# Linear attention, gate product and head norms as steps under the memory key and value tiles, output projection as tiles of each token group

## The chip, the core and the metric

The kernel runs on one core of a Trainium2 chip (trn2). The metric is the device time of one execution in microseconds; lower is better. TensorE (PE, with its weight loads PEld) multiplies, VectorE (DVE), ScalarE (ACT) and GpSimd (POOL) work element by element, SyncE (SP) issues most transfers. Each engine takes its instructions strictly in the order in which the program lists them and waits at semaphores for the others.

## What is computed

A two-layer encoder over two token groups, a prompt group of 512 tokens ("P") and a sample group of 256 ("S"), with 1024 channels and shared weights. Cut to what matters:

```python
def trunk(x, mem, p):                      # both groups, all in float32
    # layer 0: mixer = S5 state space | gated linear attention (GLA)
    u, q, k, v, og, glr = split(rms_norm(x) @ ev_w_in)
    y_s5  = s5_mixer(u, ...)               # ends: y = gelu(y); y * sigmoid(y @ w_glu)
    y_gla = gla_mixer(q, k, v, og, glr)    # two directions, chunks of 64, 4 heads of 64 x 128
    x = x + concat(y_s5, y_gla) @ ev_w_out                     # output projection
    x = x + cross_attention(rms_norm(x), rms_norm(mem), ...)   # 256 memory tokens a group, 4 heads
    x = x + square(relu(rms_norm(x) @ w1)) @ w2                # MLP, 1024 -> 4096 -> 1024
    # layer 1: differential attention, then cross attention and MLP again

def gla_mixer(...):
    g = log_sigmoid(lr @ w_gate + b_gate) / 16                 # a decay per direction and channel
    # per chunk: b = cumsum(g);  scores = tril((q e^(b-ref)) (k e^(ref-b))^T)
    #            o = scores v + (q e^b) S_prev;   S = e^(b_last) S_prev + (k e^(b_last-b))^T v
    return rms_norm(o, per head) * silu(og)
```

## The kernel before

Channels lie on the 128 partitions, tokens along the rows. A **tile** of work is one 128x128-column block of a weight matrix (512 KB) against all tokens of a group: 24 matmuls, because values and weights are split into a high and a low part and three of the four products are taken (`pe_tile`, L1757). Each weight tile is loaded by SyncE, copied to its high part by ScalarE (`high`, L1729) and subtracted to its low part by VectorE (`low`, L1734). A prompt tile has 512 moving columns, a sample tile 256.

The program has three stages, each of one or more blocks; at the end of a block all engines meet.

- `mixer_in`: the combined input projection (17 tiles) woven with the state-space mixer in four batches (`NB`). q, k, v and gates are parked in DRAM, the mixer's output y too (`store_y`, L540), and loaded back at its end (L827, L828); x is loaded again (L830).
- `s5_gla`, in blocks one after the other: the gate product (L1072, with wglu), then linear attention for the head pairs t = 0 and 1 over all 768 tokens (gates L1164, cumulative sum L1204, transposes of k L1173, chunk states L1182 and their recurrence L1225, scores L1277, masks L1302, head outputs L1285 and L1290), the sigmoid of the output gates (L1318), `head_norm_stage`, and the output projection as `product_stage` with its own weight stream (L249, L251). GpSimd does the products of q and decay (L1236) and low parts of weights (L218).
- `trunk_tail`: a list of **slots** written out at build time. A slot holds one tile, or none, and steps of other work that were queued with `later`; `drain` empties the queue into slots without a tile. Every engine walks the same list. On TensorE a slot is: scores of attention steps, the tile, the statistic of the tile before (`pe_post`), then the other steps; on ScalarE and VectorE: first parts of steps, the weight part two or three tiles ahead, the tile's evacuation (`act_tile`, `dve_tile`), the statistic of the tile before (`dve_post`, L2044 to L2046), last parts of steps. The tail begins with the sample group's cross norm, then its query tiles, memory keys and values of layer 0 (16 tiles on the 512 memory tokens, `memory(m0)`), output tiles, memory of layer 1 (16 tiles), then the sample MLP with the prompt group's query tiles and cross attention inside it, and the prompt MLP.

Norm steps have the granularity of `FINE` or `PAIRS` (channels per slot): apply (`dve_apply`, L2120), high part on ScalarE, residue on VectorE (`dve_fin`, L2127).

## Time and profile before

| | us |
|---|---|
| median of three runs (2866.41 to 2869.27) | 2867.13 |
| the profiled execution | 2867.88 |
| its span | 2866.1 |
| TensorE busy (x14044) | 2539.3, 89% |
| VectorE busy (x2658) | 1562.5, 55% |
| ScalarE busy (x1896) | 1128.5, 39% |
| GpSimd busy (x24) | 42.0, 1% |
| TensorE's share of the chain that ended last | 65% |

The span runs from the first to the last instruction of the profiled execution; the 1.8 us around it belong to the time. A matmul's busy time overlaps its neighbours', so a busy TensorE isn't one at its peak. The granted clock is the share of full speed that TensorE's clock had, one of the two levels 0.5 and 1.0 at any moment, and a mean over a window.

### The profile page before, as it was taken

Reading aid. Unit: us, or ns where it says so; the run is one execution under the profiler, and the core shown is the slowest. Engines: PE = TensorE matmul, PEld = TensorE weight load, DVE = VectorE, ACT = ScalarE, POOL = GpSimd, SP = SyncE. Lnnn points to the kernel's source line nnn. Section 1 sums busy time; section 2 is a strip of 40 time slices with the busy share of each in tenths; the row PEclk is TensorE's granted clock in tenths of the full one; section 3 lists DMA queues with packets and bytes.
Section 4 is the critical chain, followed back from the end, with each engine's and each line's share of the span. In section 5 each row is a group of like instructions: output and inputs, shape, how many; then the busy total and the mean of one; then the engine's idle time right before and its main releaser. Section 6 shows DMA issues by size and latency. Waiting matters only on the chain.

```text
span 2866.1 us, 35043 instructions
## 1 busy us (share of the span) xinstructions
PE 2539.3 (89%) x14044; PEld 2162.3 (75%) x14044; DVE 1562.5 (55%) x2658; ACT 1128.5 (39%) x1896; POOL 42.0 (1%) x24
## 2 busy tenths in 40 slices
PE   5887356656999999999999999999989999999999
PEld 3786235645878789988997798877777789888887
DVE  8798354153546555556646654465577555543333
ACT  4131011122434444535545544354556444343332
POOL 0000011020000000000000000000000000000000
PEclk9899665578999999999999999999999999999999
DMA  4222500002323432533442242322322332333332
GB/s 139 78 65 61 186 3 0 0 29 80 96 74 118 140 103 89 178 118 125 132 133 81 82 155 88 110 89 81 96 75 81 125 118 89 112 116 96 96 99 92
DMA packets 96481, 274.34 MB, mean 96 GB/s; under 512 B 18080, under 2 KB 32544, under 8 KB 94912
## 3 DMA queue, kind: packets, MB, share of 16 engines
q1 hardware_dynamic: 94016, 261.62, 29.4%
q10 hardware_dynamic: 2304, 10.49, 1.2%
q8 instruction: 112, 1.84, 0.3%
q14 instruction: 49, 0.40, 0.0%
HBM read 254.77 MB, written 15.20 MB: 94 GB/s over the span
## 4 chain that ended last, share of the span: by engine, by line
PE 65%; DVE 6%; ACT 3%; issue 1%; DMA 0%; SPq 0%; ACTq 0%; DVEq 0%
PE ps L1757 57%; PE ps L1823 2%; PE ps L1850 2%; PE ps L1892 1%; DVE wlo L1734 1%; PE ps L1868 1%; PE ps L1881 1%; ACT whi L1729 1%; PE ps L1789 1%; DVE ringP L2120 1%; DVE region_S L2173 1%; DVE ps L2045 1%; DVE ps L2044 0%; DVE region_S L2192 0%; DVE yP L2046 0%
## 5 line engine op out<-in xcount | busy, mean ns | idle before, releaser
L1734 DVE TENSOR_TENSOR wlo<-wraw,whi 128x1024 fp32r<-128x1024 f32 x416 | 505.2, 1218 | 54.8 <-ACT whi L1729 54.7
L1757 PE MATMUL ps<-in_hP,whi 128*128 128x512 f32 x1280 | 516.4, 403 | 2.5 <-issue 2.5
L1729 ACT ACTIVATE whi<-wraw 128x1024 fp32r<-128x1024 f32 x416 | 437.5, 1052 | 178.8 <-PE ps L1757 134.0
L1757 PE MATMUL ps<-in_hP,wlo 128*128 128x512 f32 x1280 | 500.1, 391 | 0.0
L1757 PE MATMUL ps<-in_lP,whi 128*128 128x512 f32 x1280 | 499.2, 390 | 0.0
L1757 PE MATMUL ps<-in_hS,whi 128*128 128x256 f32 x1024 | 306.4, 299 | 24.5 <-DVE in_lS L2127 14.8
L1757 PE MATMUL ps<-in_lS,whi 128*128 128x256 f32 x1024 | 293.8, 287 | 0.0
L1757 PE MATMUL ps<-in_hS,wlo 128*128 128x256 f32 x1024 | 293.1, 286 | 0.0
L1757 PEld LDWEIGHTS ps<-in_hP,whi 128*128 128x128 f32 x1280 | 241.0, 188 | 58.9 <-issue 8.8
L1757 PEld LDWEIGHTS ps<-in_lP,whi 128*128 128x128 f32 x1280 | 241.1, 188 | 53.7 <-issue 5.5
L1757 PEld LDWEIGHTS ps<-in_hP,wlo 128*128 128x128 f32 x1280 | 240.8, 188 | 51.9
L2065 DVE TENSOR_TENSOR x<-ps,x 128x512 f32<-128x512 f32 (+1 forms) x176 | 98.1, 557 | 314.8 <-PE ps L1757 313.7
L1757 PEld LDWEIGHTS ps<-in_hS,whi 128*128 128x128 f32 x1024 | 200.4, 196 | 42.8 <-issue 19.8
L1757 PEld LDWEIGHTS ps<-in_lS,whi 128*128 128x128 f32 x1024 | 200.8, 196 | 2.8 <-issue 2.0
L1757 PE MATMUL ps<-hid_hP,whi 128*128 128x512 f32 x512 | 202.1, 395 | 0.0
L1757 PEld LDWEIGHTS ps<-in_hS,wlo 128*128 128x128 f32 x1024 | 200.4, 196 | 0.0
L1757 PE MATMUL ps<-hid_hP,wlo 128*128 128x512 f32 x512 | 199.3, 389 | 0.0
L1757 PE MATMUL ps<-hid_lP,whi 128*128 128x512 f32 x512 | 199.3, 389 | 0.0
L2075 DVE TENSOR_TENSOR hid_lP<-ps,hid_hP 128x512 fp32r<-128x512 f32 x64 | 44.3, 692 | 234.6 <-ACT hid_hP L1969 234.6
L1967 ACT ACTIVATE ps<-ps 128x512 f32<-128x512 f32 (+1 forms) x128 | 60.7, 475 | 261.7 <-PE ps L1757 261.5
L1757 PE MATMUL ps<-hid_hS,whi 128*128 128x256 f32 x512 | 149.7, 292 | 9.2 <-DVE hid_lS L2075 5.8
L1757 PE MATMUL ps<-hid_lS,whi 128*128 128x256 f32 x512 | 145.7, 285 | 0.0
(434 smaller groups left out, 4146.5 us busy)
## 6 DMA issues: line engine op xcount, KB each, us to landing
wraw<-wt SPq DMA_DIRECT2D x416, 512.0 KB, 3.5
mix_wraw<-wt ACTq DMA_DIRECT2D x12, 512.0 KB, 4.2
raw<-wstream SPq DMA_DIRECT2D x4, 1024.0 KB, 11.0
x<-x_in SPq DMA_DIRECT2D x4, 768.0 KB, 8.5
vog<-vog_scratch SPq DMA_DIRECT2D x1, 3072.0 KB, 14.1
x<-x_in SPq DMA_DIRECT2D x1, 3072.0 KB, 12.0
mix_wraw<-wt SPq DMA_DIRECT2D x5, 512.0 KB, 10.3
mix_u<-x SPq DMA_DIRECT2D x32, 64.0 KB, 3.0
```

Of the source, the lines that this page charges most:

```text
L1729: nc.scalar.activation(whi[:, n % NHI, :, :], wraw[:, n % NRAW, :, :], ACT.Copy).then_inc(wh.sem, 1)
L1734: nc.vector.tensor_tensor(wlo[:, n % NRAW, :, :], wraw[:, n % NRAW, :, :], whi[:, n % NHI, :, :].bitcast(F32), ALU.subtract).then_inc(wr.s ...
L1757: last = nc.tensor.matmul(ps[:, m % 2, 0:N[prod.g]], w_[:, k, :], x_[:, k, :], start=(k == 0 and j == 0), stop=(k == KT - 1 and j == 2))
L1789: nc.tensor.matmul(ps[:, 2, 0:s.n], s.mat, ring[g][:, i % 2, :], start=True, stop=True).then_inc(z["ssum"].sem, 1)
L1823: last = nc.tensor.matmul(ps[:, 3 + q_ % 2, b * 256:(b + 1) * 256], qx[g][:, 2 * h + j, lo:lo + P], km[g][:, 2 * h + j, :], start=(j == 0) ...
L1850: last = nc.tensor.matmul(ps[:, 7, j * 256:(j + 1) * 256], vm[g][:, kt, (2 * h + j) * P:(2 * h + j + 1) * P], at[:, q_ % 2, kt * 256:(kt + ...
L1868: last = nc.tensor.matmul(ps[:, 3 + zz, 0:N[g]], dq[g][rows, h, b * P:(b + 1) * P], dk[g][rows, h, :], start=True, stop=True)
L1881: last = nc.tensor.transpose(ps[:, 5, j * P:(j + 1) * P], scb[g][:, q_ % 2, 0, j * P:(j + 1) * P], ident)
L1892: last = nc.tensor.matmul(ps[:, 6 + h % 2, b * P:(b + 1) * P], dv[g][:, j, h * P:(h + 1) * P], at[:, q_ % 2, j * P:(j + 1) * P], start=(j ...
L1967: act_chain(nc.scalar.activation(acc_ps, acc_ps, ACT.Relu))
L2065: nc.vector.tensor_tensor(x[:, i, cols(g)], ps[:, b, 0:N[g]], x[:, i, cols(g)], ALU.add).then_inc(tf[b].sem, 1)
L2075: nc.vector.tensor_tensor(hid_l[g][:, i, :], ps[:, b, 0:N[g]], hid_h[g][:, i, :].bitcast(F32), ALU.subtract)\
```

## The change

`s5_gla`, `product_stage`, `head_norm_stage` and all that served them are gone. `mixer_in` ends with the memory norm of layer 0 (squares and sums before the last mixer product, `dve_mem` behind it), issues the load of the memory and of the tail's first five weight tiles from ScalarE's queue after its last tile, and parks the low-rank gate input in DRAM too. The tail begins with the 16 memory tiles of layer 0, four slots without a tile, and the 16 memory tiles of layer 1. Linear attention is cut into four **units** (sample and prompt group, head pairs 0 and 1) of seven steps, one step a slot; the gate product into four groups of output columns with two steps each; each head's norm and gate into two steps. Keys and values of both layers now go through DRAM (`load_kv`). The output projection is eight sample and eight prompt tiles of the ordinary kind ("eo"); then come query tiles of both groups, output tiles, and the sample MLP's 64 tiles in one piece. From the prompt MLP of layer 0 on, the order is that of before.

```diff
-            nS, n0 = Norm("S", "cross0"), Norm("P", "mem0", mem, ymem)
-            later([("squares", nS)], *norm_steps(nS, PAIRS), [("squares", n0)])
-            drain()
-            q = Product("q", "S", WT["q0"], nS.ready)
...
+            m0 = Memory(0, None)
             memory(m0)
...
+            n1.after = m0
+            m1 = Memory(1, n1.ready)
+            scale = norm_steps(n1, PAIRS)
+            scale[0] = [("napply", n1, 0, 2)]
+            for st_ in scale[:4]:
+                slots.append((None, st_))
+            later(scale[4])
+            memory(m1)
+            gl = {g: Gla(g) for g in "SP"}
+            gl["P"].after = m1
+            units_ = [Unit(0, "S", 0, "A", 0), Unit(1, "S", 1, "A", 1536), Unit(2, "P", 0, "B", 0), Unit(3, "P", 1, "A", 0)]
+            for o in range(4):
+                attach(16 + o, [[("glu", o, 0)], [("glu", o, 1)], [("gsplit", gl["S"], o, o + 1)]])
+            for u, first in zip(units_, (1, 6, 20, 25)):
+                attach(first, [[("gla", u, k)] for k in range(7)])
+            attach(12, [[("ogload", "S", 2), ("wgluload",)]])
+            for h in range(GH):
+                attach(13 + 2 * h, [[("fin", gl["S"], h, 0)], [("fin", gl["S"], h, 1)]])
+            attach(31, [[("ogload", "P", 4), ("gsplit", gl["S"], 4, 6)], [("gsplit", gl["S"], 6, 8)], [("xload",)]])
+            for h in range(GH):
+                attach(32 + h, [[("fin", gl["P"], h, 0)], [("fin", gl["P"], h, 1)]])
+            nS = Norm("S", "cross0")
+            queue[0].append(("gsplit", gl["P"], 0, 2))
+            later(*[[("gsplit", gl["P"], k, k + 2)] for k in range(2, KT, 2)], [("kvload", "S", 0, None)], [("kvload", "P", 0, None)])
+            run(Product("res", "S", WT["eo"], gl["S"].ready, norm=nS))
+            nP = Norm("P", "cross0")
+            later([], *norm_steps(nS, PAIRS))
+            run(Product("res", "P", WT["eo"], gl["P"].ready, norm=nP))
+            q = Product("q", "S", WT["q0"], nS.ready)
+            later(*norm_steps(nP, FINE))
+            run(q)
+            qp = Product("q", "P", WT["q0"], nP.ready)
...
+            later([("qstat", q)], *cross_steps(a))
+            run(qp)
...
+            later([("qstat", qp)], *cross_steps(ap_))
+            run(Product("res", "S", WT["o0"], a.ready, norm=nS))
+            rest = [queue.popleft() for _ in range(len(queue))]
+            later(*merged(rest, norm_steps(nS, PAIRS)))
+            for _ in rest:
+                slots.append((None, queue.popleft()))
+            nP = Norm("P", "mlp0")
+            run(Product("res", "P", WT["o0"], ap_.ready, norm=nP))
             nS1 = Norm("S", "mix1")
             mS = Mlp("S", 0, nS, nS1)
...
             later([], *norm_steps(nP, FINE))
-            mS.run(16)
+            mS.run(64)
```

A unit's TensorE steps (the ScalarE and VectorE parts have the same step numbers, `act_gla` and `dve_gla`; the long middle part of step 1 comes behind the slot's tile, `act_gla_post` and `dve_gla_post`):

```diff
+            def pe_gla(pe, u, k):
+                if k == 0:
...
+                    for z in range(2):
+                        nc.tensor.matmul(ps[:, 3 + z, 0:u.n], wg[:, z, t * P:(t + 1) * P], lr[:, cols(g)], start=True, stop=True)\
+                            .then_inc(zd.sem, 1)
+                elif k == 2:
...
+                        pe.wait_ge(krd.sem, 2 * i + z + 1)
+                        for j in range(BL[g]):
+                            last = nc.tensor.transpose(ps[:, 5 + z, j * P:(j + 1) * P], u.krel[z][:, j * P:(j + 1) * P], ident)
+                elif k == 3:
+                    pe.wait_ge(ktr.sem, 2 * i + 2)
+                    pe.wait_ge(qrd.sem, 2 * i + 2)
+                    pe_scores(pe, u)
+                elif k == 4:
+                    pe.wait_ge(scr.sem, i + 1)
...
+                                last = nc.tensor.matmul(kv_ps(z, c)[DK * hh:DK * hh + DK], koT[rows, z, lo:lo + DK],
+                                                        vtok[g][rows, c // 2, h * DV:(h + 1) * DV], start=True, stop=True)
+                elif k == 5:
+                    pe.wait_ge(wrd.sem, i + 1)
+                    pe_heads(pe, u)
```

## Rows read from the trace of the kernel before

**Rows 1.** The page: busy tenths in 40 slices, and TensorE's granted clock
```profile
PE   5887356656999999999999999999989999999999
...
PEclk9899665578999999999999999999999999999999
```
**Rows 2.** Windows, stages up to 753 us: start:end, length, busy (count) by engine, PEclk, DMA share, GB/s
```profile
344.40:370.90 26.50, 22.93 (x64) 12.98 (x64) 8.46 (x8) 3.28 (x5) 0.04 (x1) 0.92 0.10 40
370.90:413.60 42.70, 13.53 (x116) 9.64 (x117) 28.13 (x38) 12.51 (x17) 13.00 (x12) 0.56 0.02 5
413.60:464.20 50.60, 46.59 (x192) 41.95 (x192) 3.78 (x4) 0.81 (x1) 0.00 (x0) 0.50 0.00 0
464.20:554.90 90.70, 59.27 (x308) 50.75 (x308) 31.91 (x42) 13.70 (x19) 9.62 (x4) 0.52 0.00 1
554.90:601.20 46.30, 11.65 (x16) 4.70 (x16) 21.64 (x24) 24.75 (x30) 0.00 (x0) 0.54 0.00 0
601.20:683.30 82.10, 71.38 (x384) 61.28 (x384) 27.11 (x24) 7.54 (x4) 19.17 (x4) 0.92 0.07 26
683.30:752.90 69.60, 41.55 (x237) 37.43 (x237) 42.56 (x70) 34.36 (x66) 0.00 (x0) 0.73 0.40 135
```
**Rows 3.** Windows of the tail, in the same columns
```profile
849.30:867.00 17.70, 10.79 (x50) 8.10 (x48) 7.53 (x15) 4.92 (x12) 0.00 (x0) 0.90 0.11 31
...
891.30:985.80 94.50, 94.50 (x423) 76.72 (x423) 48.83 (x78) 39.16 (x61) 0.00 (x0) 1.00 0.41 123
...
1080.10:1150.40 70.30, 68.61 (x458) 64.51 (x457) 41.93 (x74) 32.94 (x74) 0.00 (x0) 0.98 0.30 90
...
1222.40:1265.90 43.50, 43.50 (x194) 36.03 (x193) 17.34 (x21) 12.13 (x15) 0.00 (x0) 1.00 0.31 99
1265.90:1321.50 55.60, 49.47 (x387) 48.05 (x387) 40.36 (x58) 33.61 (x58) 0.00 (x0) 0.97 0.48 150
1321.50:2866.10 1544.60, 1503.49 (x8030) 1265.51 (x8028) 821.26 (x1404) 695.54 (x1218) 0.00 (x0) 0.99 0.33 102
1730.80:1791.90 61.10, 59.98 (x278) 50.10 (x277) 25.08 (x43) 24.06 (x47) 0.00 (x0) 1.00 0.23 70
1153.40:1222.40 69.00, 69.00 (x578) 69.00 (x577) 37.37 (x48) 34.65 (x51) 0.00 (x0) 1.00 0.60 183
```
**Rows 4.** Timeline around the mixer's end: start, length, instruction, [idle before <-releaser]
```profile
317.84 0.81 ACT L681 ACTIVATE sq<-ps 128x768 f32<-128x768 f32 x1 [40.23 <-PE ps L618]
...
321.25 0.96 DVE L782 SCALAR_TENSOR_TENSOR sq<-sq 128x768 f32<-128x768 f32 x1 [0.91 <-ACT sq L686]
...
344.39 2.07 PE L1072 MATMUL ps<-uqk,wglu_sb 128*128 128x512 f32 x2 [26.59 <-DMA wglu_sb<-wglu]
...
362.21 0.81 ACT L1084 ACTIVATE glu_t<-ps 128x768 f32<-128x768 f32 x1 [4.35 <-PE ps L1074]
```
**Rows 5.** Groups by line: xcount | busy us, mean ns of one | idle before
```profile
L1734 DVE TENSOR_TENSOR wlo<-wraw,whi 128x1024 fp32r<-128x1024 f32 x17 | 20.7, 1220 | 0.0
L2044 DVE SCALAR_TENSOR_TENSOR ps<-ps,yP 128x512 f32<-128x512 f32 x4 | 2.8, 700 | 17.8 <-ACT yP L1912 17.8
L2120 DVE SCALAR_TENSOR_TENSOR ringP<-region_P,par 128x512 f32<-128x512 f32 x8 | 5.8, 746 | 0.0
L2127 DVE TENSOR_TENSOR in_lP<-ringP,in_hP 128x512 fp32r<-128x512 f32 x8 | 5.3, 688 | 3.5 <-ACT in_hP L1984 3.3
L1204 DVE TENSOR_TENSOR_SCAN uqk<-gm,uqk 128x768 f32<-128x768 f32 x2 | 3.5, 1758 | 0.1
L1225 DVE SCALAR_TENSOR_TENSOR gl_b<-gl_b,decay,ps 128x128 f32<-128x128 f32 x40 | 11.6, 345 | 9.5 <-PE ps L1182 9.1
L1252 ACT ACTIVATE sq<-rstd 128x768 f32<-128x768 f32 x2 | 1.7, 827 | 0.0
```
**Rows 6.** Timeline of linear attention's matmuls on TensorE (rows are records, two to a matmul)
```profile
401.92 2.83 PE L1182 MATMUL ps<-vog,gl_b 64*64 64x128 f32 x48
...
413.61 5.46 PE L1277 MATMUL ps<-gl_b,krel 64*128 64x128 f32 x24 [6.61 <-PEq L1160]
```

More of the change, by code:

```diff
@@ L24 @@
 M = 512
[L25 to L28 removed]
 DEPTH = 2
 FB = 4
+NRAW = 5
+NT_MIX = 17
 EPS = 1e-6
@@ new lines, in c3, with pe_scores @@
+            def c3(a):
+                return a.rearrange("p (c i) -> p c i", i=CH)
+            def pe_scores(pe, u):
+                for z in range(2):
+                    for j in range(BL[u.g]):
+                        js = slice(j * P, (j + 1) * P)
+                        for hh in range(2):
+                            rows = slice(DK * hh, DK * hh + DK)
+                            last = nc.tensor.matmul(ps[:, 3 + 2 * hh + z, js], u.krel[z][rows, js], u.qrel[z][rows, js], start=True, stop=True)
+                last.then_inc(scd.sem, 1)
```

1125 lines of the change are left out of this document (490 added, 635 removed).

## The prediction

> **What bounds the kernel now.** I read the page's forty slices first. TensorE's row stands at 9 in nearly every slice from the eleventh on, and holds values of 3 to 8 from the fifth to the ninth; its granted clock dips to 5 to 7 in the same slices [rows 1]. So something sits between 290 and 700 us that is neither long matmul work nor at full clock.
>
> The timeline around it shows TensorE waiting 26.6 us, to 344.4 us, while the mixer's last output is stored and read back and the gate weight arrives [rows 4]. Windows cut at the stage borders tell the rest [rows 2]. The gate product takes 26.5 us. Linear attention runs from 370.9 to 554.9 us, in three windows with TensorE busy 13.5, 46.6 and 59.3 us at clocks of 0.56, 0.50 and 0.52. Gates and head norms follow, 46.3 us with 11.7 busy; then the output projection, 82.1 us; then the first norm of the tail and the sample group's query tiles, 69.6 us with 41.5 busy. Behind it the memory key and value tiles run with TensorE busy throughout at clock 1.00 [rows 3]. Inside one stage the next instruction waits for the engine before it, so no engine is the bound from 318 to 753 us; the sequence is.
>
> The second set of windows gives prices of work that stays [rows 3]. 24 sample tiles take 69.0 us, 2.88 us each, with 183 GB/s; eight prompt tiles take 43.5 us, 5.44 us each; sixteen memory tiles with their head statistics and transposes take 94.5 us, 5.9 us each. The tile list of before reaches the first tile of the prompt group's layer-0 MLP after 128 tiles, at 1321.5 us. From there both kernels run the same 288 tiles in the same order, for 1544.6 us [rows 3]. So I count both kernels to that point.
>
> **The change, step by step.** *Mixer end.* In both kernels VectorE's last step of the mixer ends at 322.2 us [rows 4]. New behind it is the memory norm's finish: a table load and Ln and Exp on ScalarE (an estimate of 3 us, from its pass of 0.83 us over 768 columns, [rows 5]), three VectorE passes of 0.70 us, then eight times an apply of 0.75 and a residue of 0.69 us [rows 5]: 3 + 2.1 + 11.5 us, to about 339 us. The squares and the eight sum matmuls of that norm lie in the 40.2 us in which ScalarE waits for the mixer's last product [rows 4]: nothing. Without that cover they would cost about 8 x 1.1 us. ScalarE's six new DMA issues (memory, five weight tiles) lie in the same wait, and SyncE's queue loses the loads of x, q, k, v and the gate's halves there. Gone from the path are the read back [rows 4], which now has the whole first memory product as cover, and the norm and the weight loads after 683.3 us. Five weight tiles are loaded already, so the first tile needs a table load, one high part and one low part (1.2 us each by the low part's row, [rows 5]), and it runs on a TensorE that was idle: first tile as if started at 345 us.
>
> *Tiles that stay tiles.* 32 memory tiles, 2 x 94.5 = 189 us.
>
> *Linear attention's matmuls.* TensorE was busy 13.5 + 46.6 + 59.3 = 119.4 us with them, at about half clock [rows 2]; at full clock 60 us. The new form has the same products, less those at the sequence edges. Value 59 us, since they now stand between tiles that run at 1.00; the other end is 118 us, if they stay at half clock.
>
> *Its VectorE and ScalarE work.* By widths from [rows 5] a prompt unit (512 columns) holds VectorE for two scans of 1.17, some sixteen passes of about 0.65, twelve state steps of 0.35 and two wide multiplications of 1.2: about 20 us; a sample unit about 11 us. Together 62 us, beside some 45 us that 16 memory tiles themselves want (48.8 us in a window of 94.5 with a norm beside, [rows 3]). ScalarE needs less. Neither is full; what counts is who waits. Each unit is seven steps in seven tile slots, and TensorE's instruction of a step stands behind that slot's tile, so a step has 5.4 us of cover. Most steps fit. The third does not: its transposes wait for k times its decay, and between the gate product and that lie bias, minimum, Exp, Ln, subtraction, scan, differences, two Exp, product, with the tile's own evacuation and statistics queued between them on both engines. For a prompt unit I sum 16 us after the gate product, against two tiles of 5.6 us: 5 us of wait. Where the slot in between also holds a key tile's head statistic on VectorE (three passes of 0.70, [rows 5], and four half-width gains, some 4 us) the wait is 10; so it is for the first sample and the second prompt unit. Waits of 6, 1, 5 and 10 us, and 2 us for each prompt unit's state chain before its head products: 26 us. Behind a waiting TensorE stand the next tiles; behind VectorE's waits stand the low parts of weights, which are issued two tiles ahead.
>
> *Head norms and gates.* Eight sum matmuls of 0.43 or 0.85 us at full clock, 5 us, and about 1 us for each in which bank 2 is not free: 13 us.
>
> *Gate product.* Four no-tile slots between the two memory products hold it. Its four groups of matmuls follow each other every 5.16 us at full clock (0.81 + 4.35, [rows 4]): 20.6 us, with the second memory norm, the sample group's norms and the sigmoid on ScalarE beside it, and about 5 us until the first tile's last input: 26 us.
>
> *Clock.* Where TensorE has waited the granted clock may fall and the next tile start slow. The gate product's start after 26.6 us of waiting cost 26.5 - 20.6 = 6 us [rows 2, 4]; for waits of 5 to 10 us I take a third of it, an estimate, and count six: 12 us (0 to 36).
>
> *Projections, queries and cross attention.* Output projection as sample tiles 23 us, plus 7: in four of them VectorE has a low part of 1.22, two residues of 0.69 and two passes of 0.4 to do, 3.4 us for a tile of 2.88, and once a head norm of 4 us: 30. As prompt tiles 44. Sample query tiles with the prompt norm beneath, where VectorE is as full: 29. Prompt query tiles with sample cross attention beneath: the same pair took 61.1 us in layer 1 [rows 3], plus 3 for the queries' sums: 64. Sample output tiles with prompt cross attention: the twelve tiles of before with it took 70.3 us [rows 3]; here eight tiles and three empty slots, 52 + 18 (the drain of before, [rows 3]): 70. Prompt output tiles 44. The sample MLP's 64 tiles, 184 us, plus 10 for the norm steps under its first tiles, as the 16 tiles of before show (55.6 against 46.1 us, [rows 3]): 194. Sum 475 us.
>
> **Sum:** 345 + 189 + 59 + 26 + 13 + 26 + 12 + 475 = 1145 us, against 1321.5: a gain of 176 us. The profiled execution took 2867.9 us against a median of 2867.1, so I take **2691 us**.
>
> **A rule weighed.** From 413.6 to 464.2 us TensorE was busy 46.6 of 50.6 us and the granted clock stood at 0.50 throughout, the lower of its two levels, 1.2 of 2.4 GHz [rows 2]. So linear attention's own matmuls, dense as they are, didn't raise it in this stage; the gate product ran at 0.92 and the tile stages at 1.00 [rows 2, 3]. The Trainium skill, "TensorE: Matmul & The Clock Gate", section "HAM oscillation — how this bites in real kernels", puts slow clocks down to idle gaps between bursts. By that rule alone this stretch would have been fast, which the row contradicts. By the row the units' share would stay slow under the tiles as well, 59 us more than my sum.
>
> **The rivals.** *Chains not covered.* VectorE and ScalarE are in order, and a step of linear attention that waits holds the tile's evacuation too. If the 62 us of VectorE and some 28 us of ScalarE work (about 34 full passes of 0.83 us, [rows 5]) were all seen by TensorE, 90 us of waiting stand in place of 26: 2755 us. For it: in the present stage every one of these steps is seen [rows 2]. Against: in the memory windows VectorE works 48.8 of 94.5 us, so it has room [rows 3]. Half-clock units give about the same, 2691 + 59 = 2750.
>
> *Matmuls in pairs.* 48 matmul records of 64 rows and 64 columns took 2.83 us and 24 records of 64 rows and 128 columns 5.46 us, all over 128 moving columns and within 12 us [rows 6]: 0.05 against 0.22 us each. The new order alternates the two heads' row halves. If these ran two at a time, half of about 40 us at full clock would go, and with waits halved the time is 2691 - 20 - 20 = 2651 us. The Trainium skill, "TensorEngine Tiling (Array Packing)", section "Tiling Modes", says that row halves work in parallel, and also that a change of mode drains the array; what such a change costs no row here shows.
>
> *Slower: the clock stays low.* If the mix of tiles and small matmuls holds TensorE at the lower level from 345 to 670 us, all TensorE work there doubles: 189 + 59 + 21 + 5 = 274 us more, 2965 us. It decides once more than 176 of these 274 us lie at the low level. Against: cross attention's small matmuls between tiles ran at 0.98 [rows 3].
>
> *The change doesn't hide anything.* If the in-order queues make each slot last as long as its chain, the 184 us of linear attention remain on the path and only the gaps go (26.6 us of read back, [rows 4], 40 of the norm stage and 15 of the projection, [rows 2]): 2786 us, still faster.
>
> **Chances.** Forecast 0.60 (its own range 2660 to 2725), chains or half clock 0.22, pairs 0.10, nothing hidden 0.05, low clock 0.03. The range that leaves out no more than 2 in 10: 2645 to 2755. Faster by over 0.2% (5.7 us, about what a measurement of this kernel tells from no change) 0.96, within 0.01, slower 0.03.
>
> **What the profile after would show.** The first tile starts near 343 us; the first 16 memory tiles last about 120 us and the second 16 about 160; between them a gap of about 26 us holds the gate product; the first tile of the output projection starts near 670 us and the prompt MLP of layer 0 near 1145. Waits of TensorE for VectorE's product of k should stand at the head of its waits in those stretches, and GpSimd should have no work. I am wrong if the memory stretches last over 350 us together, if their granted clock is below 0.9, or if the tiles behind 670 us take over 500 us, as the new order of cross attention or the loads of x and of keys and values (7 MB in few tiles) may make them.

## The result and the profile after

| | before | after |
|---|---|---|
| median, us | 2866.77 (2866.39 to 2869.27, 4 runs) | 2669.94 (2669.03 to 2670.89, 4 runs) |
| span of the profiled execution, us | 2866.1 | 2667.4 |
| TensorE busy | 89% | 93% |

The ratio is 0.931, with a 95% interval from 0.930 to 0.933: 197 us less. The forecast was 2691 us with a range from 2645 to 2755. The page of the changed kernel, first its span, the busy times, and the rows of the forty slices that answer to [rows 1]:

```profile
span 2667.4 us, 35145 instructions
PE 2467.6 (93%) x14026; PEld 2099.6 (79%) x14026; DVE 1561.9 (59%) x2747; ACT 1147.3 (43%) x1975; POOL 0.2 (0%) x4
PE   5888489888999889999999999999989999999999
PEclk9899789999999999999999999999999999999999
```

The holes between slices five and eleven are filled, and TensorE's clock no longer dips to 5 there. GpSimd has next to no work (0.2 us). The windows are cut at the first matmul of each stage's first tile (columns: window, its length, then busy time and instructions of TensorE, weight load, VectorE, ScalarE and GpSimd, granted clock, DMA share, GB/s). In order: first memory product with the two sample units; the gap with the gate product; second memory product with the two prompt units; output projection, sample and prompt; sample queries; prompt queries with the sample group's cross attention; sample output with the prompt group's; prompt output; the sample MLP; all the rest.

```profile
341.70:466.70 125.00, 118.86 (x612) 95.34 (x613) 64.97 (x127) 45.12 (x84) 0.00 (x0) 0.93 0.42 138
466.70:497.00 30.30, 24.94 (x80) 14.39 (x78) 20.52 (x36) 18.03 (x35) 0.00 (x0) 0.94 0.14 44
497.00:652.40 155.40, 136.00 (x822) 106.89 (x821) 100.21 (x168) 66.09 (x112) 0.00 (x0) 0.93 0.34 107
652.40:678.10 25.70, 24.55 (x199) 23.76 (x198) 22.21 (x35) 17.05 (x27) 0.00 (x0) 1.00 0.62 212
678.10:722.10 44.00, 44.00 (x196) 36.41 (x195) 25.23 (x42) 17.22 (x27) 0.00 (x0) 1.00 0.48 173
722.10:754.70 32.60, 28.56 (x207) 27.69 (x206) 25.61 (x34) 18.40 (x33) 0.00 (x0) 0.90 0.41 130
754.70:817.00 62.30, 62.30 (x302) 52.91 (x301) 23.88 (x40) 22.52 (x46) 0.00 (x0) 1.00 0.22 68
817.00:885.10 68.10, 59.49 (x364) 54.32 (x363) 41.61 (x83) 27.83 (x66) 0.00 (x0) 0.95 0.22 70
885.10:928.80 43.70, 43.70 (x194) 36.19 (x193) 21.22 (x30) 13.45 (x19) 0.00 (x0) 1.00 0.27 85
928.80:1122.60 193.80, 186.51 (x1539) 184.95 (x1538) 115.05 (x154) 108.63 (x178) 0.00 (x0) 1.00 0.56 174
1122.60:2667.40 1544.80, 1503.83 (x8030) 1266.23 (x8028) 820.81 (x1404) 695.37 (x1218) 0.00 (x0) 0.99 0.32 102
```

The last row stands against the 1544.6 us of [rows 3]: from the prompt group's layer-0 MLP on nothing changed. All of the gain lies ahead of that point, which came at 1321.5 us and now comes at 1122.6. In the first and third row the clock is 0.93, where linear attention alone had 0.50 to 0.56 [rows 2], though VectorE works 165 of 280 us there. TensorE's waits between 341 and 665 us (engine, line <- releaser: total, times, longest):

```profile
PE ps L1863 <- DVE region_S L1943: 10.7, 2, 6.6
PE ps L1863 <- DVE x L1943: 4.8, 1, 4.8
PE ps L2015 <- DVE yP L1603: 4.0, 1, 4.0
PE ps L1828 <- DVE region_S L1966: 3.4, 3, 2.1
...
PE ps L2015 <- DVE vtmp L1654: 2.7, 3, 1.2
```

At the head stand the transposes of a unit's third step (L1863), which wait for the product of k and its decay on VectorE (L1943), as the prediction named them. Four units have three such waits, of 4.1, 4.8 and 6.6 us; the second sample unit has none. Third is a head norm's sum, then the head products (L1828, a unit's sixth step) that wait for the states. Left out is the first tile's wait for its weight, 2.8 us.

### The profile page after: what moved, and what is told of

The parts are those of the page before. It is cut to its first block, busy times and chain, and to the rows that moved or that the text cites. A ratio compares the mean times of both kernels' runs of the same rounds, so it can differ in the third digit from the quotient of the medians.

```text
span 2667.4 us, 35145 instructions
## 1 busy us (share of the span) xinstructions
PE 2467.6 (93%) x14026; PEld 2099.6 (79%) x14026; DVE 1561.9 (59%) x2747; ACT 1147.3 (43%) x1975; POOL 0.2 (0%) x4
## 4 chain that ended last, share of the span: by engine, by line
PE 74%; DVE 9%; ACT 4%; issue 1%; ACTq 0%; DVEq 0%
PE ps L1321 63%; PE ps L1384 2%; PE ps L1409 2%; DVE wlo L1298 1%; PE ps L1451 1%; PE ps L1427 1%; PE ps L1440 1%; DVE ps L1602 1%; DVE ps L1601 1%; PE ps L1353 1%; DVE yP L1603 1%; PE ps L1828 1%; ACT yP L1470 1%; DVE region_S L1726 1%; ACT whi L1293 1%
## 5 line engine op out<-in xcount | busy, mean ns | idle before, releaser
L1321 PE MATMUL ps<-in_hP,whi 128*128 128x512 f32 x1344 | 546.9, 407 | 4.4 <-DVE wlo L1298 2.8
L1298 DVE TENSOR_TENSOR wlo<-wraw,whi 128x1024 fp32r<-128x1024 f32 x432 | 524.1, 1217 | 36.7 <-ACT whi L1293 36.4
L1293 ACT ACTIVATE whi<-wraw 128x1024 fp32r<-128x1024 f32 x432 | 454.1, 1052 | 192.5 <-PE ps L1321 133.4
L1321 PE MATMUL ps<-in_hP,wlo 128*128 128x512 f32 x1344 | 527.6, 393 | 0.0
L1321 PE MATMUL ps<-in_lP,whi 128*128 128x512 f32 x1344 | 527.2, 392 | 0.0
L1321 PE MATMUL ps<-in_hS,whi 128*128 128x256 f32 x1088 | 321.5, 296 | 8.1 <-DVE hid_lS L1634 4.3
L1321 PE MATMUL ps<-in_lS,whi 128*128 128x256 f32 x1088 | 310.4, 285 | 0.0
L1321 PE MATMUL ps<-in_hS,wlo 128*128 128x256 f32 x1088 | 310.1, 285 | 0.0
L1321 PEld LDWEIGHTS ps<-in_hP,whi 128*128 128x128 f32 x1344 | 255.2, 190 | 67.1 <-issue 10.4
L1624 DVE TENSOR_TENSOR x<-ps,x 128x256 f32<-128x256 f32 (+1 forms) x192 | 106.8, 556 | 334.9 <-PE ps L1321 333.6
L1321 PEld LDWEIGHTS ps<-in_lP,whi 128*128 128x128 f32 x1344 | 255.4, 190 | 56.5 <-issue 5.3
## 6 DMA issues: line engine op xcount, KB each, us to landing
mix_mem<-mem_in ACTq DMA_DIRECT2D x1, 2048.0 KB, 10.4
```

The lines of the kernel that those rows point to most:

```text
L1293: nc.scalar.activation(whi[:, n % NHI, :, :], wraw[:, ws(n), :, :], ACT.Copy).then_inc(wh.sem, 1)
L1298: nc.vector.tensor_tensor(wlo[:, ws(n), :, :], wraw[:, ws(n), :, :], whi[:, n % NHI, :, :].bitcast(F32), ALU.subtract).then_inc(wr.sem, 1)
L1321: last = nc.tensor.matmul(ps[:, m % 2, 0:N[prod.g]], w_[:, k, :], x_[:, k, :], start=(k == 0 and j == 0), stop=(k == KT - 1 and j == 2))
L1624: nc.vector.tensor_tensor(x[:, i, cols(g)], ps[:, b, 0:N[g]], x[:, i, cols(g)], ALU.add).then_inc(tf[b].sem, 1)
```

## The experiments

All times are medians, each kernel beside runs of the kernel before on the same chip; its ratio to that has an interval of about ±0.0013, some 4 us. The changed kernel ran a second time in the midst of them (`e5_changed_again`: 2670.7 us), so a difference is taken against 2670.

> The changed kernel as it is, once more, as the measure for the three beside it: 2670 us by every theory.

The stage times are from the timelines of the profiled executions, each the distance between the first matmuls of two tiles, in us:

| kernel | median | first tile at | first memory product and gap | second memory product | output projection | MLP of the prompt group to the end |
|---|---|---|---|---|---|---|
| changed | 2669.9 | 341.7 | 155.3 | 155.4 | 69.7 | 1544.8 |
| changed, second run | 2670.7 | 341.2 | 155.3 | 155.4 | 69.7 | 1542.4 |
| e1 halves in turn | 2696.1 | 342.6 | 162.0 | 175.3 | 69.7 | 1544.2 |
| e2 spare slot | 2677.5 | 340.4 | 151.2 | 159.5 | 76.4 | 1544.9 |
| e3 no prompt units | 2617.7 | 341.8 | 155.3 | 107.1 | 69.7 | 1545.1 |
| e4 units uncovered | 2755.2 | 341.9 | 289.2 | 108.9 | 67.6 | 1544.9 |
| e6 sample units shifted | 2656.8 | 340.4 | 142.7 | 157.9 | 69.7 | 1542.2 |
| e6b prompt unit too | 2664.4 | 343.0 | 147.6 | 156.0 | 69.7 | 1544.2 |
| e7 prompt units early | 2656.8 | 340.6 | 147.5 | 150.4 | 67.6 | 1545.1 |
| e8 head norms back | 2660.3 | 342.2 | 145.6 | 154.8 | 69.7 | 1546.0 |
| e9 scan before statistic | 2650.0 | 342.7 | 145.3 | 148.6 | 69.7 | 1542.2 |
| e10 both | 2653.8 | 342.3 | 144.9 | 152.4 | 69.7 | 1544.7 |

The last column holds the same work in every kernel and scatters by 3.8 us, the first by 2.6. A difference of medians under 4 us is therefore not read below; the stages between are, and the two runs of the changed kernel have the same three to 0.1 us. Not in the table is the stretch from the sample queries to the end of the sample MLP, 397.8 to 402.9 us.

**What the cover is worth: units in slots without a tile.**

```diff
+            for _ in range(12):
+                slots.append((None, []))
             n1 = Norm("P", "mem1", mem, ymem, stat=False)
...
+            for _ in range(12):
+                slots.append((None, []))
             later(scale[4])
             memory(m1)
...
-            for u, first in zip(units_, (1, 6, 20, 25)):
+            for u, first in zip(units_, (16, 21, 32, 37)):
```

> The changed kernel with all four units in slots without a tile: 12 such slots between the first 16 memory tiles and the gate product, 12 between the gate product and the second 16. All work is the same, only the tiles beside the steps are gone. Theory cover: without tiles every step's chain is seen by TensorE, and its clock falls to the lower level there: between 115 us (the sum of the chains) and 184 us (what linear attention took in the kernel before) instead of the 61 us that the units cost under tiles (50 of matmuls and about 11 of waits), so 55 to 120 us more, 2725 to 2790 us, with the granted clock in those slots near 0.5. Rival that the new form of the steps, not the tiles, makes them cheap: under 20 us more, below 2690 us.

Measured: 2755.2 us, ratio 0.961 (0.960 to 0.963), 85 us more than with cover. Windows of this kernel over the two sample units and over the two prompt units, then its waits of TensorE between 437 and 632 us:

```profile
437.50:498.00 60.50, 28.97 (x201) 22.91 (x198) 26.04 (x67) 11.26 (x32) 0.00 (x0) 0.53 0.15 48
536.00:631.10 95.10, 51.08 (x390) 42.80 (x390) 42.20 (x86) 17.81 (x37) 0.00 (x0) 0.54 0.00 1
```

```profile
PE ps L1868 <- DVE region_S L1948: 23.9, 3, 10.5
PE ps L1833 <- DVE region_S L1971: 19.1, 4, 6.6
PE ps L1868 <- DVE x L1948: 14.4, 1, 14.4
PE ps L1882 <- DVE scT L1927: 9.3, 4, 3.5
```

(Lines stand five further down than in the changed kernel.) Without tiles these four kinds of wait are 66.7 us, against 18.9 us of the first three with tiles and none for the masks (the last row); and the clock is 0.53 and 0.54, much as in the kernel before (0.50 to 0.56, [rows 2]). Some 13 us of the difference belong to the experiment alone: the gate product waits 7.2 us for its weight and the first prompt unit 6.0 us for an exponential of the last gate group, since no tile lies ahead of them either. So the tiles give some 70 to 85 of the 197 us: 48 by hiding the chains, and by what is left of the difference some 24 by the clock. What lowers the clock there, the longer waits or the missing tiles, the run doesn't tell, since they come together. The theory of cover stands; that the new form of the steps alone makes them cheap falls, though 112 us of the gain remain without any cover.

**What the units cost under tiles: the prompt units left out.**

```diff
-            for u, first in zip(units_, (1, 6, 20, 25)):
+            for u, first in zip(units_[:2], (1, 6)):
```

> The changed kernel without linear attention's two prompt units (seven steps each); the prompt group's head norms run on q as it was loaded. Theory that the trace shows the whole price: two prompt units cost their matmuls (16 us each), the two waits for k times decay (4.8 and 6.6), 1.3 us of waits for the state and 1.5 us each for three slow tiles: about 49 us, so about 2621 us. Rival: their VectorE and ScalarE work also delays the tiles in ways that no single wait shows: over 60 us, below 2610 us. By the prediction's terms (39 of matmuls, 15 and 4 of waits, 6 of slow tiles) it would be 64 us, 2606 us.

Measured: 2617.7 us, ratio 0.913 (0.912 to 0.914), 52 us less; the second memory product falls from 155.4 to 107.1 us, by 48. The price read from the trace (49 us) closes for that product; 2.7 us more lie behind the output projection, in the stretch that is not in the table. And the 38.5 us by which VectorE works less in that product (61.7 against 100.2) cost little beyond the waits that the trace names. This kernel leaves out half of linear attention, so only its time is of use. The prediction's own terms made it 64 us, 15 too many.

**Alternating row halves.** Scores and state products in the order of before, all of one head's 64 rows and then all of the other's:

```diff
 def pe_scores(pe, u):
-    for z in range(2):
-        for j in range(BL[u.g]):
-            for hh in range(2):
+    for hh in range(2):
+        for z in range(2):
+            for j in range(BL[u.g]):
...
 def pe_heads(pe, u):
-    for j in range(BL[u.g]):
-        ... both heads, then for z, for c, for hh: state product
+    for hh in range(2):
+        for j in range(BL[u.g]):
+            ... this head, then for z, for c: state product
```

> The changed kernel with one thing undone: scores and state products take all matmuls of one head's row half first and then all of the other's, as the kernel before did, instead of alternating the halves. Theory pairs: alternating 64-row matmuls run nearly two at a time (32 score records of a prompt unit in 2.06 us, 0.064 us each), and without alternation each takes what it took before at half clock, halved (0.114 us, 24 in 5.46 us): 96 score records and 160 state records by 0.05 us are about 13 us, so about 2683 us, with the 32 score records at about 3.6 us. Theory clock only: the records are short because TensorE now runs at full clock, and the order of the halves is of no account: 2670 us, the 32 score records still at about 2.1 us.

Measured: 2696.1 us, ratio 0.940 (0.939 to 0.942), 26 us more, twice what the theory of pairs expected and far from the other; the 32 score records take 3.50 us, where that theory said 3.6. Groups of state products of the first prompt unit (L1838) with an intra-chunk product (L1828) between them, in the changed kernel, from the timeline of TensorE; then the same with halves in turn (L1836):

```profile
548.50 0.89 PE L1838 MATMUL ps<-x,region_S 64*128 64x64 f32 x12
549.31 0.71 PE L1828 MATMUL ps<-x,region_P 128*128 128x128 f32 x4
...
550.40 1.11 PE L1838 MATMUL ps<-x,region_S 64*128 64x64 f32 x16
```

```profile
557.14 0.88 PE L1836 MATMUL ps<-x,region_S 64*128 64x64 f32 x6
557.95 0.71 PE L1828 MATMUL ps<-x,region_P 128*128 128x128 f32 x4
558.59 1.10 PE L1836 MATMUL ps<-x,region_S 64*128 64x64 f32 x8
```

Sixteen records take what eight take, at the same full clock (the intra-chunk product L1828 ahead of them has 0.71 us in both). The edit also splits the groups, so TensorE goes from full-array to half-array matmuls and back twice as often; the price of a record tells the two apart. Four records more cost 0.22 us where the halves alternate (12 and 16 records), two more cost 0.22 us where they come in turn (6 and 8). So here two 64-row matmuls in different row halves run at the same time when they follow each other, and not when one half's come first and then the other's. The Trainium skill says in "TensorEngine Tiling (Array Packing)", section "Tiling Modes", that row halves work in parallel; these rows agree. An estimate by the distances between starts: scores and head products grow by some 18 us at equal clock, where 13 were expected, the more frequent change included, and the other 8 us are clock. In the last prompt unit, from the timeline with halves in turn:

```profile
622.31 1.10 PE L1836 MATMUL ps<-region_S 64*128 64x64 f32 x8
...
627.31 1.97 PE L1836 MATMUL ps<-region_S 64*128 64x64 f32 x8
```

From about 626 us on the same eight records take 1.97 us: the lower level, in the midst of a stretch of 18.1 us in which TensorE was busy 17.7. In the changed kernel this unit's head products, done in half the time, stay at 1.00 throughout. That is worth some 4 us there, and the tiles behind the two prompt units' head products, 7.4 and 8.1 us here and 5.8 and 5.7 in the changed kernel, are worth 4 more. (The second sample unit's head products, behind a wait of 2.1 us, ran at the lower level in both kernels.) Summed over the four units, scores and state products are busy 6.4 + 12.8 = 19.3 us in the changed kernel and 10.4 + 27.9 = 38.3 us here; the intra-chunk products, of which none is a pair, rise from 15.6 to 20.3, in part by clock and in part because they come in groups of four and not of eight (5.7 us and 4.6 in the first prompt unit, at full clock in both).

**The wait for k's decay: one more slot.** An empty slot between second and third step of the first sample and the first prompt unit.

```diff
-            for u, first in zip(units_, (1, 6, 20, 25)):
-                attach(first, [[("gla", u, k)] for k in range(7)])
+            for u, first, spare in zip(units_, (0, 6, 20, 26), (1, 0, 1, 0)):
+                steps_ = [[("gla", u, k)] for k in range(7)]
+                attach(first, steps_[:2] + [[]] * spare + steps_[2:])
```

> The changed kernel with one empty slot more between the second and third step of the first sample and the first prompt unit (the sample unit starts a slot earlier for it, the last prompt unit and what follows it a slot later). Theory waits: TensorE's waits of 4.1, 4.8 and 6.6 us for k times its decay are a chain longer than two tiles; with a third tile as cover the first two go, the last falls to under 5 because no key tile's head statistic lies in it now, and two of the slow tiles behind such waits go (1.5 us each): 14 us less, about 2656 us. Rival: VectorE's whole work sets the pace and the waits come back at later steps or at the output projection, which gets its inputs a slot later: 2666 to 2676 us.

Measured: 2677.5 us, ratio 0.934 (0.933 to 0.935): slower than the changed kernel. The first memory product and gap gain 4.1 us, the second loses 4.1, the output projection 6.7. TensorE's rows from the timeline show where (lines three further down; in brackets the wait ahead and what ended it), and below them the clock of the last unit's head products:

```profile
520.88 0.66 PE L1350 MATMUL ps<-par,ringP 128*128 128x128 f32 x4 [4.08 <-DVE yP L1606]
524.42 1.94 PE L1866 MATMUL ps<-par,x 128*128 128x128 f32 x8 [2.88 <-DVE x L1946]
...
573.98 1.29 PE L1866 MATMUL ps<-par,region_S 128*128 128x128 f32 x8 [2.03 <-DVE region_S L1946]
...
602.12 1.23 PE L1831 MATMUL ps<-x,region_P 128*128 128x128 f32 x4 [4.82 <-DVE region_S L1969]
...
659.60 2.08 PE L2018 MATMUL ps<-region_S,par 128*128 128x512 f32 x2 [3.59 <-DVE vtmp L1657]
```

```profile
602.10:616.90 14.80, 14.78 (x89) 13.42 (x89) 1.70 (x2) 0.00 (x0) 0.00 (x0) 0.50 0.07 19
```

Two waits did what was expected or nearly so: the first sample unit's fell from 4.1 to 1.6 us, the last unit's from 6.6 to 2.0. In the first prompt unit a third tile of cover should have ended the wait, and 2.9 of 4.8 us are left, with 4.1 us of a new one just ahead: a value tile's transposes (L1350) that wait for the statistic on VectorE (L1606). The state's wait of the last unit, 0.4 us in the changed kernel, is 4.8; behind it the head products ran at 0.50 and took 14.8 us in place of 8.1. And a head norm now waits between tiles of the output projection. The expectation's rival is closer (2666 to 2676, just missed), but "VectorE's whole work" isn't it, since e3 found no such cost. What the new positions share is that VectorE's step comes in the slot behind the one that ends a key tile pair's **head statistic**, the mean square of one head of the memory keys from which their norm is made.

**Collision with the head statistic.** Slots 0 to 15 hold the first memory product's tiles, 16 to 19 none, 20 to 35 the second's. The statistic is finished on VectorE in the last part of slots 2, 6, 10, 14 and 22, 26, 30, 34; slot 3, 7 and so on lie behind it. In the changed kernel the third step of the first sample unit (slot 3) and of the second prompt unit (slot 27), and the sixth of the second sample unit (slot 11), lie there, and these are the waits of 4.1, 6.6 and 2.1 us. So the sample units were moved by a slot:

```diff
-            for u, first in zip(units_, (1, 6, 20, 25)):
+            for u, first in zip(units_, (0, 7, 20, 25)):
...
-                attach(13 + 2 * h, [[("fin", gl["S"], h, 0)], ...
+                attach(14 + 2 * h, [[("fin", gl["S"], h, 0)], ...
```

> The changed kernel with the first sample unit a slot earlier and the second a slot later (what follows the second moves with it). Theory collision: TensorE waits for a unit's third or sixth step when VectorE has to finish a key tile's head statistic just ahead of it, in the last part of the slot before; slots 3, 7, 11, 23, 27 and 31 lie behind such statistics. The third step of unit 0 now leaves slot 3 for slot 2 and the sixth of unit 1 leaves slot 11 for slot 12, so the waits of 4.1 and 2.1 us go, with the slow tiles behind them (1.6 and 1.5) and the half clock of unit 1's head products (3 us): about 12 us less, 2658 us. Theory length: the chain of the third step is simply longer than two tiles; then unit 0 waits 4 us in its new place as well and only the 2.1 us can go: 2666 us or more.

Measured: 2656.8 us, ratio 0.927 (0.926 to 0.928), 13 less; up to the output projection the stages give 10.1 us of it, and the rest lies in the scatter. The first sample unit's transposes, in the changed kernel and here:

```profile
372.23 0.81 PE L1863 MATMUL ps<-par,region_S 128*128 128x128 f32 x4 [4.08 <-DVE region_S L1943]
```

```profile
361.13 0.77 PE L1865 MATMUL ps<-par,region_S 128*128 128x128 f32 x4 [0.16 <-DVE region_S L1945]
```

Of the waits of 4.1 and 2.1 us nothing over 0.3 is left, with no instruction less in the chain: its length alone doesn't explain them. The sample group's head norms moved too, and two tiles behind the gap turned slow. The next run put the norms back (the load of the output gates ahead of them stayed a slot later):

```diff
-                attach(14 + 2 * h, [[("fin", gl["S"], h, 0)], ...
+                attach(13 + 2 * h, [[("fin", gl["S"], h, 0)], ...
```

> The kernel with the sample units shifted (the first a slot earlier, the second a slot later), but the sample group's head norms in the slots where the changed kernel has them, a slot earlier than in the first shifted run. There the last head norm fell under the first two tiles of the second memory product, which took 8.8 and 8.2 us instead of 5.8 and 5.7 behind waits of 2.3 and 4.0 us. Theory waits: those come from the late head norm and go: 5 us less than that run's 2656.8, so about 2651 us. Rival: they come from the shorter gap itself (25 instead of 30 us), whose norm steps are then late: no change, 2654 to 2659 us.

Measured: 2660.3 us, ratio 0.928 (0.926 to 0.929). From the first tile to the output projection it is 300.4 us, and 300.6 with the norms late: the tiles behind the gap are quick again (5.8 us each), but the gap is 31.8 us instead of 25.1. The rival's sum holds in the stages; that the shorter gap made the tiles slow isn't shown, since norms and gap moved together; the 3.5 us between the medians lie in the scattering parts.

**Order within VectorE's queue.** If the statistic ahead is the cause, it need not be moved away; the scan can go first:

```diff
+                        first = [step for step in steps if step[0] == "gla" and step[2] == 1]
+                        for step in first:
+                            dve_gla_post(v, *step[1:])
                         if before is not None:
                             dve_post(v, before)
```

> The same, and on VectorE the second half of a unit's second step (subtraction, scan, differences) stands ahead of the statistic of the tile before instead of behind it. Theory collision: ahead of the last wait for k times its decay (6.6 us) VectorE sat idle 5.9 us until ScalarE had the key tiles' root, with the scan queued behind that; with the scan first the product comes some 4 us sooner, so the wait falls from 6.6 to about 2.5 us and the tile behind it may run at full clock: 4 to 6 us less than the run before it. Theory length: the chain is the same and so is the wait; then the statistics come later instead, and the time is equal or up to 5 us longer.

Measured: 2650.0 us, ratio 0.925 (0.923 to 0.926). The stages up to the output projection give 6.5 of the 10 us. VectorE ahead of the last prompt unit's transposes, without the edit, from its timeline:

```profile
548.86 1.29 DVE L1939 SCALAR_TENSOR_TENSOR region_S<-region_S 128x512 f32<-128x512 f32 x2
555.98 0.70 DVE L1603 SCALAR_TENSOR_TENSOR ps<-ps,yP 128x512 f32<-128x512 f32 x1 [5.83 <-ACT yP L1473]
...
561.09 2.34 DVE L1981 TENSOR_TENSOR_SCAN region_S<-region_S 128x512 f32<-128x512 f32 x2
...
566.26 1.41 DVE L1945 TENSOR_TENSOR region_S<-region_P,region_S 128x512 f32<-128x512 f32 x2
```

and with it:

```profile
553.25 2.34 DVE L1981 TENSOR_TENSOR_SCAN region_S<-region_S 128x512 f32<-128x512 f32 x2
...
557.29 0.70 DVE L1603 SCALAR_TENSOR_TENSOR ps<-ps,yP 128x512 f32<-128x512 f32 x1
...
562.20 1.29 DVE L1945 TENSOR_TENSOR region_S<-region_P,region_S 128x512 f32<-128x512 f32 x2
```

VectorE stood idle 5.8 us at the statistic's first instruction, which waited for ScalarE's root, while the scan behind it could have run. In the other order the scan fills that time, the statistic comes some 1 us later and the product some 4 us sooner (the tiles ahead start 0.3 us apart in the two runs). TensorE's transposes, first without, then with the edit, and the clock of the tile behind them, in the changed kernel and with the edit:

```profile
567.09 1.94 PE L1865 MATMUL ps<-par,region_S 128*128 128x128 f32 x8 [6.60 <-DVE region_S L1945]
```

```profile
563.03 1.17 PE L1865 MATMUL ps<-par,region_S 128*128 128x128 f32 x8 [2.24 <-DVE region_S L1945]
```

```profile
578.10:585.20 7.10, 7.10 (x28) 5.76 (x27) 1.93 (x3) 1.74 (x3) 0.00 (x0) 0.79 0.14 39
```

```profile
564.00:569.70 5.70, 5.70 (x28) 4.67 (x27) 2.42 (x4) 1.79 (x3) 0.00 (x0) 1.00 0.41 132
```

The wait falls from 6.6 to 2.2 us, where 2.5 were expected, and the tile behind it runs at full clock in 5.7 us, where it took 7.1 at 0.79. The collision, not the length of the chain, made two thirds of that wait. This is the fastest of the kernels that do the whole work, 20 us below the changed one.

**Further placements, where forecasts failed.** The gate product and the first prompt unit a slot earlier, with a spare slot inside the unit:

```diff
-                attach(16 + o, [[("glu", o, 0)], ...
+                attach(15 + o, [[("glu", o, 0)], ...
-            for u, first in zip(units_, (0, 7, 20, 25)):
+            for u, first, spare in zip(units_, (0, 7, 19, 25), (0, 0, 1, 0)):
```

> The kernel of the run before, with the gate product's four groups one slot earlier (the first under the last tile of the first memory product) and the first prompt unit one slot earlier with an empty slot between its second and third step, so that its third step stays in slot 22, which no statistic precedes. Theory collision and length together: its wait of 4.8 us is chain length alone and goes with the third slot of cover, and so does a slow tile; the gap between the memory products loses one of four groups to a tile's slot but no matmul: about 7 us less than the run before, near 2651 us. Rival: as in the spare slot's run the wait comes back at another step, so no gain over the run before (within 3 us).

Measured: 2664.4 us, ratio 0.929 (0.928 to 0.930). The wait of 4.8 us went, and still nothing was gained: the gap stayed at 30.0 us, with the matmuls of all four groups in it (21.1 us; the first stands behind the last tile), the waits for ScalarE's square in the head norms rose from 1.8 to 6.2 us, and the first two tiles behind the gap took 7.8 and 7.7 us. Then without the spare slot, both prompt units and what follows them a slot earlier:

```diff
-            for u, first, spare in zip(units_, (0, 7, 19, 25), (0, 0, 1, 0)):
+            for u, first in zip(units_, (0, 7, 19, 24)):
...
-                attach(32 + h, [[("fin", gl["P"], h, 0)], ...
+                attach(31 + h, [[("fin", gl["P"], h, 0)], ...
```

> As the run before, but without the empty slot, and both prompt units, their head norms and the loads behind them one slot earlier. By the collision theory the third step of the second prompt unit now lies in slot 26, which no statistic precedes, so its wait falls from 6.6 to about 4.8 us, while the first unit's stands in the tile-less slots at 4.8 us or more; the head norms end a slot before the output projection's first tiles: between 2650 and 2658 us. By chain length alone both waits stay as they are: 2658 us or more.

Measured: 2656.8 us, ratio 0.927 (0.926 to 0.928), within what collision gave. The second unit's transposes:

```profile
557.65 1.29 PE L1865 MATMUL ps<-par,region_S 128*128 128x128 f32 x8 [2.29 <-DVE region_S L1945]
```

The wait fell from 6.6 to 2.3 us, further than the 4.8 expected, and the first unit's, expected to stay at 4.8 or more, went; the second memory product fell from 155.4 to 150.4 us and the output projection by 2.1. Last, e9 with the head norms a slot later again:

```diff
-                attach(13 + 2 * h, [[("fin", gl["S"], h, 0)], ...
+                attach(14 + 2 * h, [[("fin", gl["S"], h, 0)], ...
```

> The kernel with the scan ahead of the statistic, and the sample group's head norms a slot later again, as in the first shifted run. If the two edits are independent, the later head norms give the 3.5 us that separate the two shifted runs (2656.8 and 2660.3): 2650.0 - 3.5, about 2646.5 us. If the first prompt unit's wait of 4.8 us, which was 2.3 behind the slow tiles of the first shifted run, is already shortened by the new order on VectorE, nothing is left to gain: 2649 to 2653 us.

Measured: 2653.8 us, ratio 0.926 (0.924 to 0.927): no gain, and 3.4 us more up to the output projection, with tiles 15 and 16 at 8.1 and 8.4 us. How the head norms and the gap set each other is not settled: in e6 and e10 the gap was 25.1 us, and the tiles beside it took the gain back.

## Why the prediction held, step by step

The forecast to the layer-0 prompt MLP was 1145 us and it came at 1122.6; of the 22.4 us, 17.6 lie ahead of the output projection. None of its signs of being wrong came: the memory stretches last 280 us together (350 was the limit), their clock is 0.93 (0.9), and the tiles behind them take 470 us (500). By the terms of the sum:

| term | forecast | measured | read from |
|---|---|---|---|
| first tile | 345 | 341.7 | timeline |
| 32 tiles | 189 | about 188 | what the other rows leave of 652.4 |
| linear attention's matmuls | 59 | 52.6 | busy time of its six lines |
| waits of the chains | 26 | 18.9 | waits, L1863 and L1828 |
| head norms | 13 for all eight | 11.3 for the five outside the gap | 5.7 busy, 5.6 waiting; the other three stand in the gap's row |
| gate product's gap | 26 | 30.3 | windows |
| slow tiles | 12 | 9.2 | six tiles of 7.1 to 7.5 us over 5.74, timeline |
| projections to sample MLP | 475 | 470.2 | windows |

Two readings in it are slightly off and nothing hangs on them: TensorE's low slices are the fifth to the tenth, at 3 to 6, and 2.83 us over 48 records is 0.06 us.

**Tiles as cover.** Right. The tiles cost what they cost before, and e3 and e4 together show that the units are paid with their matmuls and few waits under tiles, and with every chain without. The rival of chains not covered priced this at 2755 us; e4, which makes it true, took 2755.2. The near equality is luck: the rival counted 64 us more of waiting and no clock, while e4 has 48 more of waiting, 13 of waits of its own, and some 24 left over that go with the lower clock. That nothing is hidden falls by the same runs.

**Linear attention's matmuls.** The size was nearly right, the reason wasn't. The term said full clock and no pairs. With halves in turn the six lines are busy 76.3 us and not 59; some 10 us of that is the part that ran at the lower level (an estimate, its rows at 0.50 to 0.88 brought to full clock), and the rest wasn't taken apart. Alternating takes 23.7 us off again. Two errors of opposite sign, some 17 and 24 us, left 6. The step that failed is the choice of 59 over the rivals: both had a part in it. The rival of pairs had the mechanism, and its 20 us for the matmuls were about what scores and state products lose (19.0 us); its total of 2651 failed since the waits weren't halved (and half of 26 is 13, not the 20 that it took off) and the clock took part of it back.

**The waits.** The place was right: third step, VectorE's product of k, at the head of the waits. The sizes forecast were 6, 1, 5 and 10 us; measured 4.1, none, 4.8 and 6.6. The head statistic was named as the reason for 6 and 10, and e6 and e9 confirm it. For the other prompt unit, whose slot has no statistic, length was the reason, and its 5 us against 4.8 is in part luck. The second prompt unit has the same chain, and where no statistic stands ahead of its scan it waits 2.0 us (e2), 2.3 (e7) and 2.2 (e9). What else the first one has shows in the changed kernel's timeline, the start of each prompt unit's product (L1855) and VectorE's first pass on it (L1934):

```profile
502.74 1.98 PE L1855 MATMUL ps<-dist,accP 32*128 32x512 f32 x4
...
507.37 1.39 DVE L1934 TENSOR_SCALAR x<-ps,par 128x512 f32<-128x512 f32 x2
...
555.47 1.98 PE L1855 MATMUL ps<-dist,accP 32*128 32x512 f32 x4
...
556.70 1.54 DVE L1934 TENSOR_SCALAR region_S<-ps,par 128x512 f32<-128x512 f32 x2 [7.61 <-PE ps L1855]
```

VectorE takes up the second unit after 1.2 us and the first after 4.6, since the last sample head norm and the rest of the gate product stand ahead in its queue. So length leaves some 2 us of wait, and the rest of the 4.8 is a queue once more, read from the trace and not tested by a run of its own (in e6b and e7 this wait went, with other waits ahead of it). Not seen by the prediction: that a statistic hurts less by its own work (three passes and four gains, 3.8 us) than by the 5.8 us for which VectorE stands at its head waiting for ScalarE's root; and that the sixth step can collide in the same way.

**Clock.** The prediction went by neither the rule that it weighed nor the row of dense work at 0.50 [rows 2], but took it that the tiles hold the level up; the level was 0.93, against 0.53 and 0.54 in e4's slots without tiles. The rival of a clock that stays low is refuted. The 12 us for slow tiles stand at 9.2.

**Gap.** 26 us forecast, 30.3 measured. The matmuls took 12.1 + 10.5 us and not 20.6, since the first half started slow again; and beside them stand waits of 1.2, 2.4 and 1.8 us for a head norm, a transpose and another head norm, with their small matmuls, 7.7 us where I had 5.

**Behind the output projection.** Right within 5 us in 475. The sample tiles of the projection took 25.7 us and not 30; the sample queries 32.6 and not 29, with TensorE idle 4 of them.

**What the run leaves open.** How the 112 us that e4 kept split between the read back that went, the pairs, the earlier norms and the projection as tiles was not taken apart by runs; the order of the halves alone is 26 of it at most, measured under tiles. The windows say where the 199 us up to the prompt MLP lie. From the gate product to the head norms it was 256.8 us [rows 2], with two memory products, taken at 94.5 each [rows 3], 445.8, and is 310.7: 135 us, of which e4 gives the tiles 70 to 85. The output projection went from 82.1 to 69.7: 12 us. The first tile starts 3 us ahead of the old gate product. The other 49 lie behind the projection, where TensorE was busy 41.6 of 69.6 us ahead of the old first memory product and 10.8 of 17.7 behind it [rows 2, 3].

## What to carry to other kernels

Small dependent steps are best costed under a big tile by what they make the bottleneck engine wait for, not by what they keep the others busy: the prompt units' 38.5 us on VectorE cost TensorE only the waits that its rows show. Ahead of each such wait, read the queue of the engine that releases it: an instruction that stands idle at the head for a third engine can cost more than its own work (5.8 us against 3.8 here), and exchanging the two orders gained where another slot of distance lost. And a wait that is taken away in one slot can come back where the shifted steps land, so a schedule is best moved one unit at a time, with the stages compared and not the total alone.

## What the hardware showed that was not expected

Alternating 64-row matmuls of two row halves ran two at a time (16 records in 1.11 us against 8 in 1.10), with full-array matmuls between the groups. Going from the one to the other costs little here, an estimate of 0.1 us: groups of 12 and 16 start 0.81 and 1.04 us ahead of what follows them, 0.06 us a record, and so much is left. TensorE's granted clock fell to the lower level, 1.2 of 2.4 GHz, in the midst of dense work where the 64-row matmuls came one at a time (17.7 of 18.1 us busy, mean 0.76); and it stayed there through the head products, alternating ones, that followed a wait of 4.8 us (14.8 of 14.8 us busy, 0.50). The Trainium skill, "TensorE: Matmul & The Clock Gate", section "HAM oscillation — how this bites in real kernels", puts slow clocks down to idle gaps; the second row begins with one, the first does not.
